# Decoder trunk on one core: some weight remainders and gate products move to GpSimd, dots and coefficient groups are placed anew

## The reference, cut to what matters

```python
def peer(h, w_query, sub_keys, u_tab, v_tab):
    q = (xt @ w_query).reshape(T, 8, 2, 128)
    s = jnp.einsum('thpd,hpnd->thpn', q, sub_keys)
    s_half, i_half = lax.top_k(s, 16)
    cand_s = s_half[:, :, 0, :, None] + s_half[:, :, 1, None, :]      # 16 x 16 sums
    top_s, pos = lax.top_k(cand_s, 16)
    ids = take(i_half[0] * 128 + i_half[1], pos)
    gates = jax.nn.softmax(top_s, axis=-1)
    a = gelu(einsum('chkd,cd->chk', u_tab[ids], x))
    return einsum('chk,chkd->cd', gates * a, v_tab[ids])
```

## Time and profile before

| | us |
|---|---|
| median of 3 runs | 3477.5 (3471.12 to 3483.51) |
| the profiled execution, device time | 3496.24 |
| its span, from first to last instruction | 3494.4 |
| TensorE busy | 3328.6 (95%) |
| VectorE busy | 2984.3 (85%) |
| ScalarE busy | 2191.8 (63%) |
| GpSimd busy | 1330.3 (38%) |
| mean DMA traffic | 249 GB/s |

### The profile page before, as it was taken

The page is one execution under the profiler, slowest core; times in us unless marked ns, Lnnn a source line. Parts: engine busy times, 40 slices in busy tenths (PEclk is TensorE's granted clock), DMA queues, the critical chain, the costliest instruction groups (busy, mean ns, idle before and its releaser), DMA issues.

```text
span 3494.4 us, 63120 instructions
## 1 busy us (share of the span) xinstructions
PE 3328.6 (95%) x19278; PEld 2443.3 (70%) x19278; DVE 2984.3 (85%) x6039; ACT 2191.8 (63%) x3118; POOL 1330.3 (38%) x1126
## 2 busy tenths in 40 slices
PE   6999999999999999999989999999999998999999
PEld 5767775667777667767777677666677776676776
DVE  6899777998888778888869997789988886888888
ACT  3574435567777666777746724455677776766776
POOL 0000017316555556557500000271265564555554
PEclk9999999999999999999999999999999999999999
DMA  5312272459999999999923123535699999999998
GB/s 199 103 61 69 89 264 97 156 190 326 363 354 331 319 353 345 363 350 359 339 81 90 61 79 121 211 115 179 221 335 361 345 341 310 360 355 351 344 361 296
DMA packets 421669, 868.89 MB, mean 249 GB/s; under 512 B 167824, under 2 KB 233360, under 8 KB 421008
## 3 DMA queue, kind: packets, MB, share of 16 engines
q1 hardware_dynamic: 310512, 544.87, 46.3%
q0 software_dynamic: 73728, 268.47, 21.3%
q10 hardware_dynamic: 37152, 52.45, 4.1%
HBM read 774.41 MB, written 85.98 MB: 246 GB/s over the span
## 4 chain that ended last, share of the span: by engine, by line
PE 40%; issue 26%; DVE 15%; POOL 10%; DMA 4%; ACT 3%; DVEq 0%; POOLq 0%; SPq 0%; ACTq 0%
PE ps L924 9%; PE ps L927 8%; PE ps L928 8%; POOL gbuf L586 6%; POOL spare L600 5%; PE ps L636 4%; PE ps L638 3%; PE ps L637 3%; DVE yT L1506 3%; DVE i L1752 2%; DMA raw<-stream 2%; DVE v L1748 1%; DVE S_ring L1758 1%; DMA gbuf<-u_rows,ids_u 1%; PE ps L670 1%
## 5 line engine op out<-in xcount | busy, mean ns | idle before, releaser
L670 PE MATMUL ps<-h,w 128*128 128x384 f16 (+1 forms) x2272 | 760.0, 335 | 40.1 <-ACT w L1012 40.0
L671 PE MATMUL ps<-h,w 128*128 128x384 f16 (+1 forms) x2272 | 756.8, 334 | 0.0
L1012 ACT ACTIVATE w<-w_hi 128x1024 f16<-128x1024 f32 x544 | 572.5, 1052 | 286.3 <-DVE w L1934 174.5
L600 POOL TENSOR_TENSOR spare<-spare 128x1 f32<-128x1 f32 x504 | 393.9, 782 | 909.2 <-DVE a_sp L1740 500.9
L927 PE MATMUL ps<-cf,w 128*128 128x384 f16 x2032 | 665.2, 328 | 0.0
L928 PE MATMUL ps<-cf,w 128*128 128x384 f16 x2032 | 662.2, 327 | 0.0
L667 PE MATMUL ps<-h_hi,w_hi 128*128 128x384 f32 (+1 forms) x2272 | 489.9, 357 | 0.0
L924 PE MATMUL ps<-cf_hi,w_hi 128*128 128x384 f32 x2032 | 430.6, 354 | 23.6 <-DVE cf L1928 23.6
L1934 DVE SCALAR_TENSOR_TENSOR w<-raw,w_hi 128x1024 f16<-128x1024 f32 x256 | 313.3, 1224 | 132.8 <-ACT w_hi L1007 113.6
L667 PEld LDWEIGHTS ps<-h_hi,w_hi 128*128 128x128 f32 x2272 | 396.0, 189 | 17.4 <-issue 0.3
L1000 ACT ACTIVATE w_hi<-raw 128x1024 fp32r<-128x1024 f32 x296 | 313.7, 1060 | 144.6 <-DMA raw<-stream 105.5
(11 more groups left out here) (286 smaller groups left out, 6241.7 us busy)
## 6 DMA issues: line engine op xcount, KB each, us to landing
raw<-stream SPq DMA_DIRECT2D x682, 512.0 KB, 5.6
gelu_scratch<-g_out ACTq DMA_DIRECT2D x256, 192.0 KB, 6.0
cg<-gelu_scratch SPq DMA_DIRECT2D x256, 192.0 KB, 6.8
c_scratch<-stage SPq DMA_DIRECT2D x128, 256.0 KB
cg<-c_scratch SPq DMA_DIRECT2D x256, 128.0 KB, 5.7
qT<-ada SPq DMA_DIRECT2D x32, 512.0 KB, 6.2
cgate<-ada SPq DMA_DIRECT2D x32, 512.0 KB, 5.4
w_rows<-ada SPq DMA_DIRECT2D x32, 512.0 KB, 6.4
```

The lines of the kernel that those rows point to most:

```text
L600: nc.gpsimd.tensor_tensor(spare[:, 16:17], spare[:, 17:18], spare[:, 18:19], ALU.add).then_inc(room, 1)
L670: nc.tensor.matmul(ps[:, b, 0:n], w16[:, s, 0, c], h16[:, c, 1, t0:T], start=False, stop=False)
L671: mm = nc.tensor.matmul(ps[:, b, 0:n], w16[:, s, 1, c], h16[:, c, 0, t0:T], start=False, stop=c == C - 1)
L1012: nc.scalar.mul(w16[:, s, 1], w_hi[:, s].bitcast(F32), X_DOWN).then_inc(w16_done, 1)
```

## The change

GpSimd makes the remainders of 27 U tiles (`POOL_U`: 0 to 5, 7, 8, 10, 11, 13 and every odd one from 15 to 45) and counts them on a semaphore of its own (`pool_low`); the other 101 stay on VectorE. VectorE's remainders in the routes are placed by `low_mark`, a function of the tile, in place of one for every 3000 marked ns, and from tile 18 each is followed by one or two dots (`route_dots`). The gathers for them stand between GpSimd's remainders. GpSimd makes `gated_lo` of each group, after `one_j`, and TensorE waits for it with a semaphore (`gated_low_done`). The groups lie at tiles 48 to 118, 1.5 tiles apart (before 1.77). Two waits that ordered the common counter, one on GpSimd and one on VectorE, each with a one-element instruction behind it, go. The transposes follow tile 45, ScalarE's Exp stands before tile 38.

```diff
-U_ROUTE = 28
-U_POOL = 4
-LOW_EVERY = 3000
-C_FIRST, C_TILES = 33, 85
+U_ROUTE, U_ROWS = 40, 15
+POOL_U = (0, 1, 2, 3, 4, 5, 7, 8, 10, 11, 13) + tuple(range(U_ROWS, 46, 2))
+RT_TILE = 45
+C_FIRST, C_TILES = 48, 72
-STORE_TILES = 12
+STORE_TILES = 11
-EXP_TILE = 27
+EXP_TILE = 38
-DOTS_FIRST, DOTS_BY_GROUP = 4, 114
+DOTS_FIRST, DOTS_BY_GROUP = 22, 97
+def low_mark(u):
+
+    return 2690 * (u - 5.5) if u < U_ROWS else 28000 + 1807 * (u - U_ROWS - 0.9)
+
+
+def route_dots(u):
+
+    return 0 if u < U_ROWS + 3 else 1 + u // 2 % 2
...
             with pool.Fori(0, DEPTH) as l:
-                def low16(s, i):
+                def low16(s, i, nth):
...
                     nc.gpsimd.tensor_tensor(w16[:, s, 0], raw[:, s], w_hi[:, s].bitcast(F32),
-                                            ALU.subtract).then_inc(lo_done, 1)
+                                            ALU.subtract).then_inc(pool_low, 1)
...
-                pool.wait_ge(lo_done, l * NT + I_QRY + 4)
-                nc.gpsimd.tensor_tensor(spare[:, 15:16], spare[:, 17:18], spare[:, 18:19], ALU.add)
...
-                for u in range(U_POOL):
-                    low16(u % 4, I_U + u)
-                pool.wait_ge(ids_in, l + 1)
-                pool.wait_ge(row_used, l * 2 * P + SLOTS)
-                nc.gpsimd.tensor_tensor(spare[:, 14:15], spare[:, 17:18], spare[:, 18:19], ALU.add)
-                for n in range(SLOTS):
-                    gather(n)
-                for n in range(SLOTS, 2 * P):
+                def next_gather(n):
+
                     pool.wait_ge(room, l * (2 * P - SLOTS) + n - SLOTS + 1)
                     pool.wait_ge(row_used, l * 2 * P + n + 1)
                     nc.gpsimd.tensor_tensor(spare[:, 16:17], spare[:, 17:18], spare[:, 18:19], ALU.add).then_inc(room, 1)
                     gather(n)
+
+                def gated_low(g):
+
+                    pool.wait_ge(j_done, l * GROUPS + g + 1)
+                    nc.gpsimd.tensor_tensor(gated_lo[:, g % 2], one_j[:, g % 2], spread_out(gate_lo, g),
+                                            ALU.mult).then_inc(gated_low_done, 1)
+
+                gathers = 0
+                for nth, u in enumerate(POOL_U):
+                    low16(u % 4, I_U + u, 2 * C + nth)
+                    if u == 13:
+                        pool.wait_ge(ids_in, l + 1)
+                        pool.wait_ge(row_used, l * 2 * P + SLOTS)
+                        nc.gpsimd.tensor_tensor(spare[:, 14:15], spare[:, 17:18], spare[:, 18:19], ALU.add)
+                        for n in range(SLOTS):
+                            gather(n)
+                        gathers = SLOTS
+                    for k in range(route_dots(u - 1) if u - 1 >= U_ROWS and gathers else 0):
+                        next_gather(gathers)
+                        gathers += 1
+                while gathers < DOTS_FIRST + SLOTS:
+                    next_gather(gathers)
+                    gathers += 1
+                for g in range(GROUPS):
+                    gated_low(g)
+                    while gathers < dots_by(g + 1) + SLOTS:
+                        next_gather(gathers)
+                        gathers += 1
+                for n in range(gathers, 2 * P):
+                    next_gather(n)
...
                 def c_group(g):
 
                     pe.wait_ge(lr_done, l * GROUPS + g + 1)
+                    pe.wait_ge(gated_low_done, l * GROUPS + g + 1)
...
-                    if u == U_ROUTE + 2:
+                    if u == RT_TILE:
                         pe.wait_ge(rt_ready, l + 1)
...
-                lows = [U_POOL]
-                spent = [LOW_EVERY]
+                own_lows = [u for u in range(NKEYS) if u not in POOL_U]
+                spent = [0]
...
-                    if ns and spent[0] >= LOW_EVERY:
-                        spent[0] -= LOW_EVERY
+                    if ns and spent[0] >= low_mark(own_lows[0]):
+                        routed_rows = route_dots(own_lows[0])
                         u_low()
+                        for k in range(routed_rows):
+                            if dots[0] == 0:
+                                dve.wait_ge(h_ev, 2 * l + 2)
+                            dot()
...
-                dve.wait_ge(lo_done, l * NT + I_U + U_POOL + 4)
-                nc.vector.memset(spare[:, 0:1], 0.0)
...
                     dve.wait_ge(j_done, l * GROUPS + g + 1)
-                    nc.vector.tensor_tensor(gated_hi[:, g % 2], one_j[:, g % 2], spread_out(gate_hi, g), ALU.mult)
-                    nc.vector.tensor_tensor(gated_lo[:, g % 2], one_j[:, g % 2], spread_out(gate_lo, g),
+                    nc.vector.tensor_tensor(gated_hi[:, g % 2], one_j[:, g % 2], spread_out(gate_hi, g),
                                             ALU.mult).then_inc(lr_done, 1)
```

More of the change, by code:

```diff
@@ L83, with pooled, lows_to, pool_lows_to @@
 NE = I_W
+NPL = 2 * C + len(POOL_U)
+NL = NT - NPL
+def pooled(i):
+    return I_QRY <= i < I_U or i - I_U in POOL_U
+def lows_to(i):
+    return sum(not pooled(k) for k in range(i + 1))
+def pool_lows_to(i):
+    return sum(pooled(k) for k in range(i + 1))
 O_GN = 0
@@ L323, in build_trunk @@
         lo_done = sem("lo_done")
+        pool_low = sem("pool_low")
         w16_done = sem("w16_done")
@@ L421, in build_trunk @@
         j_done = sem("j_done")
+        gated_low_done = sem("gated_low_done")
         h_tr = sem("h_tr")
@@ L431, in build_trunk, with spread_out @@
         y_tr = sem("y_tr")
+        cube = [P, GROUP // 2, NKEYS, 2]
+        def spread_out(x, g):
+            return x[:, GROUP * g:GROUP * (g + 1)].rearrange("k (a o b) -> k a o b", o=1, b=2).broadcast_to(cube)
         v_rows = stream.rearrange("n p c q -> (n p) (c q)")
@@ L577, in _ @@
                 for i in (I_QRY + 2, I_QRY + 3):
[L578 removed]
+                    low16(i % 4, i, i - I_QRY)
                 with pool.Fori(I_QRY // 4 + 1, I_U // 4) as r:
                     for s in range(4):
[L581 removed]
+                        low16(s, 4 * r + s, 4 * r + s - I_QRY)
                 def gather(n):
@@ L630, in product @@
                     pe.wait_ge(bank_read[b], e)
-                    pe.wait_ge(lo_done, g + 5)
+                    pe.wait_ge(lo_done, n_low + 5)
                     for c in range(C):
@@ L644, in first_pair @@
                         pe.wait_ge(bank_read[q], l * (NE // 2) + i // 2 + 1)
-                    pe.wait_ge(lo_done, l * NT + i + 6)
+                    pe.wait_ge(lo_done, l * NL + i + 6)
                     for c in range(C):
@@ L1007, in high_in, with half_word @@
                     nc.scalar.mul(w_hi[:, s], raw[:, s], W_UP).then_inc(hi_done, 1)
-                def half_word(s, g):
-                    act.wait_ge(lo_done, g + 5)
+                def half_word(s, low, count):
+                    act.wait_ge(low, count)
                     nc.scalar.mul(w16[:, s, 1], w_hi[:, s].bitcast(F32), X_DOWN).then_inc(w16_done, 1)
                 def half_word_at(i):
-                    half_word(i % 4, l * NT + i)
+                    if pooled(i):
+                        half_word(i % 4, pool_low, l * NPL + pool_lows_to(i))
+                    else:
+                        half_word(i % 4, lo_done, l * NL + lows_to(i) + 4)
                 def token_root(b):
@@ L1302, in _ @@
                         coef_high((s + 1) % 4, r + (s + 1) // 4)
-                        half_word((s + 1) % 4, l * NT + I_W + 4 * r + s + 1)
+                        half_word((s + 1) % 4, lo_done, l * NL + lows_to(I_W + s + 1) + 4 + 4 * r)
                         high_in((s + 2) % 4, I_W + s + 2, r)
@@ L1866, in _ @@
                 assert count[0] == TOP_STEPS, count[0]
-                while lows[0] < U_ROUTE + 3:
+                while own_lows[0] <= RT_TILE + 1:
                     u_low()
                 dve.wait_ge(h_ev, 2 * l + 2)
-                for n in range(DOTS_FIRST):
+                while dots[0] < DOTS_FIRST:
                     dot()
-                    if n == 1:
+                    if dots[0] == DOTS_FIRST - 1:
                         u_low()
@@ L1883, in _ @@
                 dve.wait_ge(rt_ev, (l + 1) * NBD)
-                cube = [P, GROUP // 2, NKEYS, 2]
-                def spread_out(x, g):
-                    return x[:, GROUP * g:GROUP * (g + 1)].rearrange("k (a o b) -> k a o b", o=1, b=2).broadcast_to(cube)
                 for g in range(GROUPS):
-                    while lows[0] <= min(group_tile(g) + 1, NKEYS - 1):
+                    while own_lows and own_lows[0] <= group_tile(g) + 1:
                         u_low()
@@ L1902, in _ @@
                         dot()
-                while lows[0] < NKEYS:
+                while own_lows:
                     u_low()
```

17 lines of the change are left out of this document (8 added, 9 removed).

## The result

The changed kernel takes 3650.7 us (3645.93 to 3653.43, 4 runs) against 3479.45 of the kernel before in the same comparison: ratio 1.049, 95% interval 1.047 to 1.052. By the medians that is 171 us. The forecast had the side and the engine right (slower, by what GpSimd does to VectorE) and the size wrong: 3567, range to 3640. The profiled execution has a span of 3650.0 us, 155.6 more than before. The 16 us between 171 and 155.6 come from the execution that was profiled before: it lay 17 us over its median, the one after lay 1 us over its own. What made it longer is not known.

The account below looks back on a forecast made before the run. VectorE was taken to bound the routes, with TensorE, DMA and VectorE within some 15% in the groups. Routes +5 and groups +46 us a layer, rounded to +45, two layers +90, gave 3567 us; range 3440 to 3640.

Parts of the forecast that it names:

- What bounds the kernel now: U tiles: VectorE bounds the routes; in the groups TensorE, DMA and VectorE lie within some 15% of each other.
- Part one: First 48 tiles, 27 remainders on GpSimd: gain of up to 17 us eaten; tile 48 comes 5 us later a layer.
- the lock: GpSimd elementwise and VectorE two-SBUF-operand instructions run one after the other; their times add, 166 us in tiles 5 to 43.
- Part two, the lock: Groups from tile 48: gated_lo on GpSimd puts 1.89 us on VectorE's cadence, takes 0.60 off; 8.0 us a group, +46.
- Part two, the wait: Groups: TensorE's new wait for gated_lo shows only as part of the cadence, as VectorE is up to a group ahead.
- The sum: Whole kernel: each layer +5 + 46 = +51 us, rounded down to +45; two layers +90, median 3567.
- (a): Rival, both stretches: the exclusion hardly costs, GpSimd fits VectorE's idle time and top-16 work; -15 a layer, 3447; chance 0.20.
- (b): Rival, groups: gated_lo takes near 1.06 us; routes +5 and groups +8, 3500; chance 0.13.
- (c): Rival, groups: GpSimd's queue becomes the bound, 9.0 us a group, stretch +94, 3670; chance 0.10.
- (d): Rival: the change alters less than it says, ScalarE's high parts giving VectorE's order anyway; 3478; chance 0.07.
- The signs to look for: Trace after: remainder, dot and cube means 1.6 us or more, VectorE over 92%, DMA under 0.93, long-stretch spacing 5.2 or more.

Follow-up runs that it names:

- e5: Changed kernel with gated_lo and the remainders of tiles 4 to 127 back on VectorE, new places kept: 3462.0 us, ratio 0.9936.
- e1: Changed kernel with gated_lo of every group back on VectorE, all else kept: 3533.3 us, ratio 1.014.
- e9: Changed kernel with VectorE's one_j a group earlier and the gathers that a group's dots release behind the next gated_lo: 3565.8 us, ratio 1.023.
- e2: Changed kernel with TensorE multiplying with gated_hi twice and not waiting for gated_lo, which GpSimd still makes: 3592.9 us, ratio 1.031.
- e8: Changed kernel with the remainders of tiles 4 to 127 back on VectorE, gated_lo still on GpSimd: 3583.1 us, ratio 1.029.
- e6: Changed kernel with gated_lo on VectorE and GpSimd's remainder in one instruction, scaling by 256 left out: 3459.6 us, ratio 0.993.
- e4: Changed kernel with the gathers that a group's dots release put behind the next group's gated_lo: 3707.7 us, ratio 1.064.
- e3: Changed kernel with GpSimd's gated_lo cut to one element, its queue place kept, TensorE multiplying with gated_hi twice: 3528.8 us, ratio 1.013.

## Why the prediction was wrong in size, point by point

- **What bounds the kernel now**: right. TensorE's needs (4.03 and 0.89 us) make 193 and 328 us of the two stretches, and e5 came to 199 and 341.
- **Part one**: +5 us for tile 48, measured +10 (+13 in the second layer), inside the ends. The gain is there as worked out: without the lock the 48 tiles should take 218.7 - 17 = 202 us, and e5 takes 199. What was too small is the price of the lock, 22 a layer in the sum, 30 (after against e5) to 36 (e1 against e5) on the chip. Left out were three small groups with two operands (L1842, L1817 and L1820, 5 us by the trace before) and VectorE's one-operand casts: L1863 took 0.22 us in the kernel before (there L1801) and 1.29 here, L1885 0.43 (L1823) and 1.37, together 8 us more. That these are the missing 8 to 14 is not shown.
- **Part two, the lock**: right. 1.89 us for gated_lo (1.90 at the least), 1.7 a group put on VectorE, 7.6 a group when nothing else is late (e9). The 402 us at the upper end of the working were measured, but they stood there for a gated_lo of 2.35 us without lateness; that they agree is chance.
- **Part two, the wait**: the step that failed is "this wait shows only as part of the cadence". It was costed at nothing, on the ground that VectorE is up to a group ahead. The buffers allow a group, but the lead was never that long, and the trace of the kernel before could have told it. There the last cube ended 0.1 to 1.9 us before its group began on TensorE, 0.7 on average over the 48 groups; in this one 0.13 us:

```profile
875.95 0.68 DVE L1899 TENSOR_TENSOR gated_lo<-one_j,gate_lo 128x1024 f16<-128x1024 f16 x1
```

```profile
876.76 0.23 PE L895 MATMUL ps<-gated_hi,one_i 128*128 128x128 f16 x1
```

  In this order VectorE does not get further ahead, as its next remainder needs a high part that ScalarE makes behind TensorE (38.0 us of such waits before, 32.5 after). And every second group falls one tile after the last, with two gathers in GpSimd's queue: 2.0 us from one_j to the start of gated_lo and 2.0 for itself, where the lead was under 2. The wait costs 28 us a layer by e2 and up to 43 by e9 (with what the order saves in the lock), 56 to 86 of the 171.
- **The sum**: forecast +45 a layer, measured +75 in the first layer of the profiled execution. The 30 between them: 5 from part one; 23 from the group stretch, 401.7 where I had 379, or 8.5 us a group for 8.0 (of this 8.5, 7.6 stay in e9 and 0.9 are what its order takes away, where I had allowed 0.3 for waits and 0.1 by rounding up); 6 from rounding +51 down to +45, on the ground that idle time "must be given back before any of it costs"; less 4 from the base, read a tile short. Of VectorE's idle time in the stretch, 56 us before, 40 were still there after: the loop makes them, and they are no reserve. By the medians another 8 us a layer are missing: I had taken off 18.7 us because the profiled execution of before lay that far over its median, and after it lay over it by 1.
- **Rivals**: (a) fell: the means of L1804, L1775 and L1954 rose, and the first 48 tiles did not shrink. (b) fell by the 1.90 us. (c) came out closest in time (3670) and wrong in its mechanism: GpSimd is busy for 309 of 402 us. It isn't full, it is late at the wrong moment, and e9 mends most of this with the same instructions. VectorE waited only 3.1 us for rows in the stretch, the sign that (c) had named. (d) fell.
- **The signs to look for**: means of 1.6 us or more were said for the remainders, the dots and the cubes; gated_hi has 1.63 and the dots 1.56, but the remainders 1.27 and one_j and one_i 0.68, as GpSimd works at one place of the group only. Single ones over 2.5 us are there. Tile spacing 5.66 (5.2 or more), VectorE's share 90% (over 92 was said), DMA share 0.89 (under 0.93), first 48 tiles 4.8 a tile (4.4 to 4.8).

Left open: in part one, how much is VectorE held up and how much GpSimd's remainders coming late (18.9 and 41.9 us of ScalarE's waits). Nothing was found that takes one away without the other. In the stretch after, the granted clock is 0.97, in e9's and e5's 1.00; part of the 43 us may be that, at most 0.03 x 402 = 12 if TensorE was the bound all the time. e8 speaks against it: with 0.94 in the same stretch it took 403.3 us, the changed kernel 401.7.

## What to carry to other kernels

This case suggests the following. Before work goes to GpSimd, add its time to VectorE's time in instructions with two SBUF operands, as if both ran on one engine: an instruction of 1.14 us that becomes 4.24 there must free nearly four times its own time in something that doesn't collide (with 2.35 us, in e6, it cost nothing). Then place the moved operation in its queue: if it is waited for in order by the engine that sets the pace, look at what stands ahead of it at the moment its input is ready, and read the real lead from the trace (here 0.7 us), not the lead that the buffers would allow. Here, placing the work anew on VectorE alone (e5) gave the first 48 tiles what offloading was to give.

## What the runs showed of the hardware

- Small VectorE casts with one operand in SBUF are held up too: L1863, 128 elements, 0.22 us before and 1.29 on average beside GpSimd's remainders, while MAX8 and FIND_INDEX8 keep their 0.25. Of the eight L1863 in the two layers, the four that start inside one of GpSimd's take 2.36 us on average and the other four 0.22; the 58 MAX8 (t<-cand) that start inside one take 0.25 like the other 70. A blocked one ends some 0.08 us after the L597 in which it started, as here:

```profile
764.75 2.36 DVE L1863 CAST parts<-p 128x128 f32<-128x128 uint32 x1
```

```profile
764.68 2.35 POOL L597 TENSOR_TENSOR w<-raw,w_hi 128x1024 f16<-128x1024 f32 x1
```

  The Trainium skill, page "SBUF — State Buffer", section "SBUF: two separate sides", names VectorE's 2-port perf modes beside two SBUF inputs as what is shut out. The casts agree with it, though no row here shows the mode that a cast runs in.
- GpSimd gains nothing from 16-bit operands in this multiplication: 1.90 us at the least for 1024 elements, 1.89 with 32-bit ones, where VectorE needs 0.68 and 1.22.
- The granted TensorE clock was lower where TensorE stopped more: 0.974 over the whole span against 0.985 before; in the stretch 0.97 in the changed kernel, 0.94 in e8 and 0.95 in e4, where TensorE's longest stops are 3.5 to 7.8 us, and 1.00 in e1, e3, e5 and e9. 1.00 is the full level, 2.4 GHz; the lower means are that level with short times at 1.2 GHz.
